# A mixture-of-experts block table: products moved to ScalarE, one sum split in two, the first gather moved up a stage

## The reference, cut to what matters

```
expert_id, gate_w = two experts and two shares per token     # 4096 assignments
order  = argsort(expert_id)                                  # assignments by expert
dest   = start of the expert's padded run + place in it      # runs padded to blocks of 128
slot_tok[dest] = token;  slot_w[dest] = share                # the block table
for each block of 128 slots, with its expert e:
    xb = h[slot_tok[block]]                                  # gather 128 rows
    y  = (silu(xb @ w_gate[e]) * (xb @ w_up[e])) @ w_down[e]
    out[slot_tok[block]] += slot_w[block] * y                # scatter-add
```

## Time and profile before

| what | us |
|---|---|
| median of 3 runs (2533.58 to 2534.29) | 2533.66 |
| the profiled execution, its own time | 2532.34 |
| its span, first to last instruction | 2530.6 |
| TensorE busy | 2334.9 (92% of the span) |
| VectorE busy | 1325.4 (52%) |
| ScalarE busy | 995.8 (39%) |
| GpSimd busy | 482.2 (19%) |

### The profile page before, as it was taken

How to read it: one execution, slowest core, us unless ns; L and a number is a source line. 1 busy time by engine, 2 the same in 40 slices (tenths; PEclk the granted TensorE clock), 3 DMA queues, 4 the chain that set the end, 5 groups by cost and what they waited for, 6 DMA issues and landing times. The chain is left out here.

```text
span 2530.6 us, 39501 instructions
## 1 busy us (share of the span) xinstructions
PE 2334.9 (92%) x13361; PEld 1996.6 (79%) x13362; DVE 1325.4 (52%) x1763; ACT 995.8 (39%) x1642; POOL 482.2 (19%) x376
## 2 busy tenths in 40 slices
PE   3999999999999988999989994999999999999990
PEld 2788888887888877886768883888999999999990
DVE  6763232222111118886743546986866284656646
ACT  4300000000101105565433222886867385756743
POOL 0011111111212212100016442111222121212210
PEclk9999999999999998999999996999999999999995
DMA  7124422322447546437966424999999498888968
GB/s 266 50 70 146 145 103 99 133 67 75 165 143 254 177 151 209 164 103 246 300 195 212 156 109 161 342 355 347 306 316 291 130 347 261 259 244 256 291 207 315
DMA packets 312857, 516.61 MB, mean 204 GB/s; under 512 B 23485, under 2 KB 228821, under 8 KB 303448
## 3 DMA queue, kind: packets, MB, share of 16 engines
q1 hardware_dynamic: 282122, 418.81, 48.7%
q0 software_dynamic: 18000, 65.54, 10.1%
q10 hardware_dynamic: 12672, 31.46, 3.2%
HBM read 385.50 MB, written 130.24 MB: 204 GB/s over the span
## 5 line engine op out<-in xcount | busy, mean ns | idle before, releaser
L330 PE MATMUL proj_psum<-h_hi,proj_w_hi 128*128 128x512 f32 x1216 | 484.9, 399 | 11.1 <-DVE h_lo L432 10.1
L331 PE MATMUL proj_psum<-h_lo,proj_w_hi 128*128 128x512 f32 x1216 | 482.9, 397 | 0.0
L332 PE MATMUL proj_psum<-h_hi,proj_w_lo 128*128 128x512 f32 x1216 | 482.6, 397 | 0.0
L490 DVE COPY proj_out<-proj_psum 128x512 f32<-128x512 f32 x152 | 123.0, 814 | 599.5 <-PE proj_psum L332 598.6
L1837 PE MATMUL moe_p_gu<-moe_hi_gu,moe_xT_hi 128*128 128x256 f32 x1504 | 428.4, 285 | 1.2 <-DVE moe_xT_lo L1963 1.2
L1838 PE MATMUL moe_p_gu<-moe_lo_gu,moe_xT_hi 128*128 128x256 f32 x1504 | 424.1, 282 | 0.0
L1839 PE MATMUL moe_p_gu<-moe_hi_gu,moe_xT_lo 128*128 128x256 f32 x1504 | 424.0, 282 | 0.0
L1743 DVE TENSOR_TENSOR moe_lo_gu<-raw_gu,moe_hi_gu 128x1024 fp32r<-128x1024 f32 x256 | 302.8, 1223 | 45.6 <-ACT moe_hi_gu L1737 45.6
L1837 PEld LDWEIGHTS moe_p_gu<-moe_hi_gu,moe_xT_hi 128*128 128x128 f32 x1504 | 286.2, 190 | 3.5 <-issue 1.6
L1838 PEld LDWEIGHTS moe_p_gu<-moe_lo_gu,moe_xT_hi 128*128 128x128 f32 x1504 | 286.4, 190 | 2.1
L1839 PEld LDWEIGHTS moe_p_gu<-moe_hi_gu,moe_xT_lo 128*128 128x128 f32 x1504 | 286.0, 190 | 0.0
(11 more groups left out here) (301 smaller groups left out, 3574.8 us busy)
## 6 DMA issues: line engine op xcount, KB each, us to landing
raw_gu<-in_w_exp_gate SPq DMA_DIRECT2D x256, 256.0 KB, 6.7
raw_gu<-in_w_exp_up SPq DMA_DIRECT2D x256, 256.0 KB, 7.1
raw_d<-in_w_exp_down SPq DMA_DIRECT2D x128, 512.0 KB, 10.0
projected<-proj_out SPq DMA_DIRECT2D x38, 1024.0 KB, 4.2
proj_raw<-in_w_in SPq DMA_DIRECT2D x38, 512.0 KB, 10.8
proj_w_rest<-in_w_ada SPq DMA_DIRECT2D x8, 2048.0 KB, 9.7
y_sum<-proj_w_rest SPq DMA_DIRECT2D x20, 512.0 KB, 9.5
out_cut<-proj_cut ACTq DMA_DIRECT2D x32, 256.0 KB, 2.9
```

Source lines behind the costliest of these rows:

```text
L330: pe.matmul(bank, w_hi[:, u, k, :], h_hi[:, k, tok], start=(k == 0), stop=False)
L331: pe.matmul(bank, w_hi[:, u, k, :], h_lo[:, k, tok], start=False, stop=False)
L332: return pe.matmul(bank, w_lo[:, u, k, :], h_hi[:, k, tok], start=False, stop=(k == KD - 1))
L490: ins = dve.tensor_copy(view[:, ds(tg * per, per), :], psum[:, u, tg, :].rearrange("p (m r) -> p m r", r=dilation))
```

## The change

Five edits, in `route` and at the head of `experts`. (1) The five VectorE instructions of the shares go from ahead of `over` to behind the second `is_low`. (2) ScalarE multiplies the token numbers, one group of 64 columns after another, each with its own semaphore count; TensorE sums these 64 columns in `p_rows`, waiting for each group on its own. (3) The shares get a sum of their own, `p_share`, which TensorE starts after the turned table: ScalarE multiplies the first 16 groups behind its token products, GpSimd the second 16 in one instruction. (4) GpSimd copies the first token numbers and issues the first gather in `route`, ahead of that multiplication, and waits for it at the end of the stage; `row` and `xg` are allocated outside `experts`. VectorE reads `slot_rows` first and builds `entries` behind it. (5) In `experts` the first `take_x` half stands ahead of the first cut on ScalarE and VectorE, and TensorE's wait for a gather stands in the block.

```diff
 # route, GpSimd
-                for c in range(T2):
-                    pool.wait_ge(matched, c + 1)
-                    rows = is_high[:, ds(c * L, L), :]
-                    pool.tensor_tensor(value[:, ds(c * L, L), 0:NB], rows, token[:, :].unsqueeze(2).to_broadcast([P, L, NB]), ALU.mult
-                                       ).then_inc(high_ready, 1)
+                pool.wait_ge(rows_ready, 1)
+                pool.tensor_copy(row[:, :], slot_rows[:, 0:1]).then_inc(row_ready, 1)
+                pool.wait_ge(row_ready, 1)
+                pool.sem_inc(row_seen, 1)
+                pool.indirect_dma_start(out=xg[:, :], out_offset=None, in_=h_dram,
+                                        in_offset=bass.IndirectOffsetOnAxis(ap=row[:, 0:1], axis=0)).then_inc(first_gathered, 16)
+                pool.wait_ge(shares_made, 1)
+                pool.wait_ge(matched, 2)
+                pool.tensor_tensor(value[:, ds(L, L), NB:2 * NB], is_high[:, ds(L, L), :],
+                                   share[:, 1, :].unsqueeze(2).to_broadcast([P, L, NB]), ALU.mult).then_inc(second_shares, 1)
+                pool.wait_ge(first_gathered, 16)
                 pool.wait_ge(made, 2)
 # route, TensorE
                     if n % L == 0:
                         pe.wait_ge(low_ready, n // L + 1)
-                        pe.wait_ge(high_ready, n // L + 1)
-                        pe.wait_ge(shares_ready, n // L + 1)
-                    mm = pe.matmul(p_rows[:, 0:2 * NB], is_low[:, n, :], value[:, n, :], start=(n == 0), stop=(n == T2 * L - 1))
+                    pe.wait_ge(tokens_ready, n + 1)
+                    mm = pe.matmul(p_rows[:, 0:NB], is_low[:, n, :], value[:, n, 0:NB], start=(n == 0), stop=(n == T2 * L - 1))
...
                 mm.then_inc(table_turned, 1)
+                pe.wait_ge(second_shares, 1)
+                for n in list(range(L, T2 * L)) + list(range(L)):
+                    if n < L:
+                        pe.wait_ge(first_shares, n + 1)
+                    mm = pe.matmul(p_share[:, 0:NB], is_low[:, n, :], value[:, n, NB:2 * NB], start=(n == L), stop=(n == L - 1))
+                mm.then_inc(shares_summed, 1)
 # route, ScalarE
-                for c in range(T2):
-                    act.wait_ge(matched, c + 1)
-                    for t in range(L):
-                        ins = nc.scalar.activation(value[:, c * L + t, NB:2 * NB], is_high[:, c * L + t, :], ACT.Copy,
-                                                   scale=share[:, c, t:t + 1])
-                    ins.then_inc(shares_ready, 1)
+                for n in range(T2 * L):
+                    if n % L == 0:
+                        act.wait_ge(matched, n // L + 1)
+                    nc.scalar.activation(value[:, n, 0:NB], is_high[:, n, :], ACT.Copy, scale=token[:, n % L:n % L + 1]
+                                         ).then_inc(tokens_ready, 1)
+                act.wait_ge(shares_made, 1)
+                for n in range(L):
+                    nc.scalar.activation(value[:, n, NB:2 * NB], is_high[:, n, :], ACT.Copy, scale=share[:, 0, n:n + 1]
+                                         ).then_inc(first_shares, 1)
 # route, VectorE: gsum, d, gsum, share, share moved from here ...
                 dve.wait_ge(ranked, 1)
                 chain.link(tt(over[:, :, :], ...
 # ... to behind the second is_low
+                dve.sem_inc(shares_made, 1)
+                dve.wait_ge(rows_summed, 1)
+                dve.tensor_scalar(slot_rows[:, 0:NB], p_rows[:, 0:NB], -1.0, 0.0, ALU.add, ALU.max).then_inc(rows_ready, 1)
...
-                dve.tensor_copy(slot_share[:, :], p_rows[:, ds(NB, NB)]).then_inc(rows_ready, 1)
...
+                dve.wait_ge(shares_summed, 1)
+                dve.tensor_copy(slot_share[:, :], p_share[:, 0:NB]).then_inc(share_ready, 1)
 # experts
-                gather(0)                                     # GpSimd
...
+                take_x(0, 0)                                  # ScalarE and VectorE
                 for g in range(PARTS):
                     cut_high(act, g, 1, None)
                     if g == 1:
-                        take_x(0, 0)
                         take_x(1, 0)
```

More of the change, by code:

```diff
@@ L1474, in x1_part, with route @@
     return raw_gu[:, t, :, :, :].rearrange("p m k f -> p (m k f)") if t < GU else raw_d[:, t - GU, :]
-def route(nc, logits, choice, ident, table, slot_rows, slot_place, slot_share, raw_gu, raw_d, w_gate, w_up, w_down):
+def route(nc, logits, choice, ident, table, slot_rows, slot_place, slot_share, raw_gu, raw_d, w_gate, w_up, w_down, h_dram, row, xg):
     L, T2 = TILES, 2
@@ L1510, in route @@
         blk = s.sb("blk", [P, 1])
[L1511 to L1515, removed]
+        p_rank, p_total, p_rows, p_share, p_table = (s.ps(n, [P, 512]) for n in ("p_rank", "p_total", "p_rows", "p_share", "p_table"))
+        (made, consts, steps, shifted, exped, picked, ranked, index_ready, low_ready, matched, tokens_ready, shares_made, first_shares,
+         second_shares, rows_summed, shares_summed, share_ready, rows_ready, entries_ready, table_turned, table_ready, first_loaded,
+         row_ready, row_seen, first_gathered) = (s.sem(n) for n in (
+             "made", "consts", "steps", "shifted", "exped", "picked", "ranked", "index_ready", "low_ready", "matched", "tokens_ready",
+             "shares_made", "first_shares", "second_shares", "rows_summed", "shares_summed", "share_ready", "rows_ready", "entries_ready",
+             "table_turned", "table_ready", "first_loaded", "row_ready", "row_seen", "first_gathered"))
         def over_experts(a, n=NE):
@@ L1596, in _ @@
                 dve.wait_ge(consts, 1)
[L1597 to L1602, removed]
                 dve.wait_ge(ranked, 1)
@@ L1634, in _ @@
                                       iota_p[:, :].unsqueeze(1).to_broadcast([P, L, P]), ALU.is_equal).then_inc(low_ready, 1)
+                dve.wait_ge(exped, 2)
+                chain.link(dve.tensor_reduce(gsum[:, :], gexp[:, :, :], AX.X, ALU.add))
+                chain.link(dve.tensor_scalar(d[:, :], ex[:, :], 1.0, None, ALU.add))
+                chain.link(tt(gsum[:, :], gsum[:, :], d[:, :], ALU.mult))
+                chain.link(dve.reciprocal(share[:, 0, :], gsum[:, :]))
+                chain.link(tt(share[:, 1, :], share[:, 0, :], ex[:, :], ALU.mult))
+                dve.sem_inc(shares_made, 1)
+                dve.wait_ge(rows_summed, 1)
+                dve.tensor_scalar(slot_rows[:, 0:NB], p_rows[:, 0:NB], -1.0, 0.0, ALU.add, ALU.max).then_inc(rows_ready, 1)
                 every = ds(0, NB + 1)
@@ L1645, in _ @@
                 dve.tensor_scalar(entries[:, 2:3], entries[:, 2:3], -1.0, None, ALU.add).then_inc(entries_ready, 1)
[L1646 to L1648 removed]
                 dve.tensor_copy(found[:, :], p_rows[:, 0:NB]).then_inc(rows_ready, 1)
                 chain.link(dve.tensor_scalar(place[:, :], p_rows[:, 0:NB], 0.0, dummy[:, 0:1], ALU.is_equal, ALU.mult))
[L1651 removed]
+                dve.wait_ge(rows_ready, 2)
                 dve.scalar_tensor_tensor(out=slot_place[:, :], in0=place[:, :], scalar=-1.0, in1=found[:, :],
@@ L1657, in _ @@
                 dve.tensor_copy(table[:, 3, 0:1], now[0:1, NE - 1:NE]).then_inc(table_ready, 1)
-                dve.wait_ge(rows_ready, 4)
+                dve.wait_ge(shares_summed, 1)
+                dve.tensor_copy(slot_share[:, :], p_share[:, 0:NB]).then_inc(share_ready, 1)
+                dve.wait_ge(rows_ready, 3)
                 dve.wait_ge(table_ready, 2)
+                dve.wait_ge(share_ready, 1)
 def experts(nc, table, slot_rows, slot_place, slot_share, ident, h_dram, raw_gu, raw_d, w_gate, w_up, w_down, y_sum, x1_dram,
-            gate_dram, out):
+            gate_dram, out, row, xg):
     RING = 8
@@ L1673, in experts @@
         hi_d, lo_d = s.sb("hi_d", [P, KE, D], F32R), s.sb("lo_d", [P, KE, D], F32R)
-        row, place, spare = s.sb("row", [P, 1], I32), s.sb("place", [P, 1], I32), s.sb("spare", [P, 1], I32)
-        xg = s.sb("xg", [P, D])
+        place, spare = s.sb("place", [P, 1], I32), s.sb("spare", [P, 1], I32)
         xT_hi, xT_lo = s.sb("xT_hi", [P, KD, P], F32R), s.sb("xT_lo", [P, KD, P], F32R)
@@ L1998, in block_of @@
                     cuts(range(4, PARTS))
+                take_x(0, 0)
                 for g in range(PARTS):
@@ L2080, in build @@
             raw_gu, raw_d = top("raw_gu", [P, GU, 2, 2, H2], side="right"), top("raw_d", [P, KE, D], side="right")
-            route(nc, logits, choice, ident, table, slot_rows, slot_place, slot_share, raw_gu, raw_d, w_exp_gate, w_exp_up, w_exp_down)
+            row, xg = top("row", [P, 1], I32, side="right"), top("xg", [P, D], side="right")
+            route(nc, logits, choice, ident, table, slot_rows, slot_place, slot_share, raw_gu, raw_d, w_exp_gate, w_exp_up, w_exp_down,
+                  h_dram, row, xg)
         experts(nc, table, slot_rows, slot_place, slot_share, ident, h_dram, raw_gu, raw_d, w_exp_gate, w_exp_up, w_exp_down,
```

(2 more changed lines are left out.)

5 lines of the change are left out of this document (3 added, 2 removed).

## The result

The changed kernel takes 2546.74 us (median of 4 runs, 2541.69 to 2550.91) and the kernel before 2533.62 on the same chip (4 runs, 2529.59 to 2534.29): ratio 1.0059, 95% interval 1.0042 to 1.0077. That is 13.1 us slower by the medians (14.9 by the ratio), where 6.6 were forecast. The direction was right, the time lies above the range. The profiled execution is the shortest of the four (2541.69 us, span 2540.0).

The account below looks back on a forecast made before the run. Bound: VectorE's chain in `route`, the weight stream at the head of `experts`, then TensorE to the end. 2532.34 - 1.2 - 1.7 + 13.0 - 3.5 = 2538.9, plus 1.32: 2540.3 us, 6.6 slower; range 2535.5 to 2544.5.

Parts of the forecast that it names:

- shares moved back: In `route`, five VectorE instructions and their wait for ScalarE's exponentials leave the path to `over`: gain 1.2 us.
- GpSimd's products go: In `route`, each `is_low` loses 1.7 us without GpSimd's products beside it; TensorE waits for the first: gain 1.7 us.
- ScalarE's products, waits: In `route`, 32 token products covered by `is_low`, and TensorE's 32 waits already satisfied: cost 0, upper bound 9 us.
- row sums, 64 columns: TensorE's 64 records in `route` save nothing by the narrower width: 9.0 us again, bounds 7.2 to 10.
- shares' own sum: TensorE's 64 more records before `route` closes, hidden by nothing, at the 1.2 GHz level again: 9.0 us, bounds 7.2 and 10.
- head, by the weights: At the head of `experts`, weight loads no longer held back by late `lo` cuts: gain 3.5 us, bounds 0 and 4.2.
- (c): No lock: the `is_low` in `route` stay at 3.95 us; +8.3, 2542.0 us; chance 0.10.
- (a): Weight stream in `experts` catches up before 1750, so the first block's chain remains: +4.55, 2538.2 us; chance 0.18.
- ScalarE's waits before `raw_d`: Sign in `experts` that the forecast is right: ScalarE's weight waits there come earlier than 1660.
- (b): Warm shares: TensorE stays at 2.4 GHz over the gap, shares' sum 7.2 us: +4.8, 2538.5 us; chance 0.11.
- (d): Waits between TensorE's matmuls cost 0.1 to 0.28 us for each of 48: +5 to 13 more, near 2549; chance 0.04.
- (e): 64-column matmuls take half the pace of 128, each sum 5.3 us: -0.8, 2532.9 us; chance 0.07.

Follow-up runs that it names:

- the kernel with both sums wide: Changed kernel, but both sums stream 128 columns (64 of them zeros) and GpSimd makes the second shares before its wait for the rows: 2535.65 us, ratio 1.0010.
- place-only: Kernel before with one edit, the gather's two tiles (`row`, `xg`) placed ahead of the stage on the other side of SBUF: 2527.82 us, ratio 0.9982.
- the pair with the head back: Both sums of 128 columns and GpSimd's product early, without and with the head of `experts` as before (tiles keep their new place): ratios 1.0010 and 1.0011.

## Why the prediction was wrong, step by step

| step | predicted | measured |
|---|---|---|
| shares moved back | -1.2 | `over` 1.90 to 0.72 behind the first instruction: -1.2 |
| GpSimd's products go | -1.7 | row sums start 16.31 to 13.42: -2.9 with the step above, so -1.7 |
| ScalarE's products, waits | 0 | 0 |
| row sums, 64 columns | 9.0 | 13.9 |
| to the start of the shares | 5.2 | 4.45 |
| shares' own sum | 9.0 | 13.9 |
| to the start of `experts` | 1.3 | 1.45 |
| start of `experts` | +10.1 | +19.3 |
| head, by the weights | -3.5 | -3.1 |
| place of the tiles | not seen | -4.1 |
| sum | +6.6 | +12.1 |

The runs give 13.1 and 12.0 by the medians (14.9 and 12.9 by the ratios). (The profiled pair differs by 9.4: the 2.24 us by which this execution reached the stage sooner belong to it.)

**The step that failed** is the clock in "Row sums of 64 columns" and "The shares' own sum". For the second I wrote that I expect "the 1.2 GHz level again and take 9.0 (bounds 7.2 and 10)": I carried over the whole duration of the earlier trace rows, of which only a quarter of the records ran at 1.2 GHz, as if the clock had to rise after as long a time in a sum of half the columns. It never rose, and no rival on record had it stay down. The trace of the kernel before held the right upper bound: 16 records in 3.36 us at 1.2 GHz make 13.4 for 64, not 10. With 13.9 for both sums the same working gives 16.4 us slower, and with the tiles' place 12.3. The Trainium skill ("TensorE: Matmul & The Clock Gate", section "What's actually happening") says that activity releases the clock from its lower state. The runs agree for the row sums of 128 columns, in all eleven of which the clock rose, and not for those of 64: seven sums, each without a pause for 13.9 us, stayed at 1.2 GHz.

**Right:** the two gains ahead of the sums, to a tenth; the covered products; the gap to the shares within 0.8; the close of the stage; and the head. GpSimd and VectorE did wait for each other: `is_low` fell from 3.95 to 2.28 us each, so rival (c) falls. The same shows from the other side in the changed kernel, where `slot_place` (0.23 us before) takes 2.60 beside GpSimd's product; with the product earlier, as in the kernel with both sums wide, it takes 0.23 again. That the weight stream carries the shift is borne out by its packets, and rival (a), that the stream gives way, falls. The gain there was near the size worked out (3.1 us against the execution before, 2.3 against place-only's, and 1.2 in the pair with the head back). SP's load came 1.0 us later than I had it: two of SP's reads of the loop's table took 1.03 and 0.54 us in place of 0.28 each. One sign on record was wrong by its own sum: ScalarE's waits before `raw_d` were to come earlier than 1660, but a stream shifted by 6.6 us brings them later, and the first stands at 1676.5 (before: 1663.6).

**Rivals.** (b), warm shares, went the other way in the changed kernel, and was what the kernel with both sums wide showed (7.41). (d): the sum takes 13.91 us with 32 waits and 13.89 with two, so waits cost nothing. (e): at 2.4 GHz 64 columns take 7.36 us, with the weight loads busy for 7.22 of them, and 128 columns 7.41, so the weight loads set the pace, as the earlier trace rows had it.

**What was not in the prediction:** the new place of `row` and `xg` had no term in it. It was worth 4.1 us, nearly all in TensorE's pace, and hid a quarter of the loss. Without it the forecast would have been further off.

**What stays open:** why the records of 64 columns leave the clock down, and which tile's address sets the pace. The runs of one kernel spread over some 9 us. Of the 5.8 us between the two profiled executions of the changed kernel, 4.0 arise ahead of the stage's first instruction (1541.69 and 1545.64), in code that no edit here touches. The gain of the head is smaller than that spread, and only its size in the weights (1 to 3 us) is shown, not its worth in time.

## What to carry to other kernels

Price a TensorE sum from rows at the clock level it will have, and take the all-1.2-GHz price as the upper bound: here half the columns saved nothing and cost the clock. Splitting a sum in two adds a whole second pass of weight loads; the second one was also the only thing the stage waited for. And when an edit moves a tile, compare the pace of untouched loops before and after: a few ns per matmul over thousands of them can outweigh the edit itself.

## What the runs showed of the hardware

- 64-column records against 128x128 weights did not raise the clock from 1.2 GHz in 13.9 us without a pause (seven sums in four executions); with 128 columns it rose 3.4 to 6.1 us into every row sum (eleven executions; 9.0 to 10.3 us in all).
- Once at 2.4 GHz, the clock outlasted 7.4 us of 64-column records (one execution). Over a gap of 2.0 us with 0.4 us of work it held in two executions and fell in one, at the start of the next sum; over 4.4 us with 0.5 us of work it fell (one execution).
- The place of tiles in SBUF changed the pace of the same gate and up matmuls (128x256) from 117 to 113 ns a record.
- A VectorE instruction with two operands from SBUF was held up beside a GpSimd product: 128x2048 took 3.95 us beside it and 2.28 without, 128x64 took 2.60 in place of 0.23.
